# Prompt attention: the value product split over column halves of TensorE, its softmax sums over column quarters

## The reference

```python
s = jnp.einsum('bqgrd,bgqnjd->bgrqnj', qb, kg)          # selected blocks
p = masked_softmax(s - slopes * dist, m_s, axes=(-2, -1))
o_s = jnp.einsum('bgrqnj,bgqnjd->bqgrd', p, vg)
...
p_w = masked_softmax(s_w - slopes * dist_w, m_w, axes=-1)  # window of 512
o_w = jnp.einsum('bgrqk,bkgd->bqgrd', p_w, vwb)
...
o = gt[..., 0:1] * o_c + gt[..., 1:2] * o_s + gt[..., 2:3] * o_w
```

## Time and profile before

| | us |
|---|---|
| Median of 3 runs | 2069.13 (2068.73 to 2072.95) |
| Profiled execution, its own time | 2070.01 |
| Its span in the profile | 2068.1 |
| TensorE busy | 1850.6 (89% of the span) |
| VectorE busy | 866.3 (42%) |
| ScalarE busy | 541.1 (26%) |
| Mean granted clock | 0.938 |
| Value product L1939, 128 keys, busy | 139.9 |

### The profile page before, as it was taken

One profiled execution on the slowest core, in us unless ns is written; L12 is line 12 of the kernel. 1 busy time (PEld: TensorE's weight loads), 2 busy tenths in 40 slices (PEclk: granted clock), 3 DMA queues, 4 the chain that ended last, 5 costly groups with the idle time before them and its releaser, 6 DMA issues. The chain is left out here.

```text
span 2068.1 us, 27935 instructions
## 1 busy us (share of the span) xinstructions
PE 1850.6 (89%) x11698; PEld 1576.6 (76%) x11698; DVE 866.3 (42%) x1540; ACT 541.1 (26%) x1001; POOL 223.7 (11%) x285
## 2 busy tenths in 40 slices
PE   2799989948887687899999898899999999999997
PEld 2798889937777675555555687899999999999996
DVE  4634161123333434454443453444444444444446
ACT  3221221132222124444444322211211111122112
POOL 0200000022232101001100000100011011110000
PEclk9999999969999666999999999999999999999999
DMA  4000013030000200000000301111111111111102
GB/s 120 23 24 30 13 53 133 15 95 2 2 2 29 62 1 25 1 1 21 21 0 1 127 1 41 62 41 41 41 43 60 41 41 41 41 41 41 41 31 87
DMA packets 31503, 79.50 MB, mean 38 GB/s; under 512 B 11390, under 2 KB 17870, under 8 KB 26098
## 3 DMA queue, kind: packets, MB, share of 16 engines
q1 hardware_dynamic: 31314, 77.63, 11.1%
q0 software_dynamic: 64, 0.09, 0.0%
HBM read 69.62 MB, written 10.12 MB: 39 GB/s over the span
## 5 line engine op out<-in xcount | busy, mean ns | idle before, releaser
L266 PE MATMUL ps<-mix_hi,wbuf 128*128 128x364 f32 (+1 forms) x768 | 254.1, 331 | 9.5 <-DVE wbuf L2703 6.1
L267 PE MATMUL ps<-mix_lo,wbuf 128*128 128x364 f32 (+1 forms) x768 | 253.6, 330 | 0.0
L268 PE MATMUL ps<-mix_hi,wbuf 128*128 128x364 f32 (+1 forms) x768 | 253.6, 330 | 0.0
L2739 DVE TENSOR_TENSOR x<-x,ps 128x512 f32<-128x512 f32 (+1 forms) x288 | 190.6, 684 | 120.2 <-PE ps L268 120.2
L266 PE MATMUL ps<-wbuf,mlp_hid_hi 128*128 128x512 f32 x576 | 225.3, 391 | 4.4 <-DVE wbuf L2703 4.4
L267 PE MATMUL ps<-wbuf,mlp_hid_hi 128*128 128x512 f32 x576 | 225.2, 391 | 0.0
L268 PE MATMUL ps<-wbuf,mlp_hid_lo 128*128 128x512 f32 x576 | 225.0, 391 | 0.0
L2725 DVE TENSOR_TENSOR mlp_hid_lo<-mlp_rect,mlp_hid_hi 128x364 fp32r<-128x364 f32 (+1 forms) x96 | 75.2, 783 | 290.0 <-ACT mlp_hid_hi L2646 290.0
L266 PEld LDWEIGHTS ps<-mix_hi,wbuf 128*128 128x128 f32 x768 | 146.2, 190 | 10.5 <-DVE wbuf L2703 6.4
L2697 POOL TENSOR_TENSOR mlp_rect<-mlp_rect 128x364 f32<-128x364 f32 (+1 forms) x96 | 76.0, 791 | 661.3 <-ACT mlp_rect L2668 661.3
L267 PEld LDWEIGHTS ps<-mix_lo,wbuf 128*128 128x128 f32 x768 | 145.8, 190 | 0.5
(11 more groups left out here) (536 smaller groups left out, 3494.2 us busy)
## 6 DMA issues: line engine op xcount, KB each, us to landing
out_raw<-in_w_up SPq DMA_DIRECT2D x16, 1024.0 KB, 4.8
mlp_raw_down<-in_w_down SPq DMA_DIRECT2D x16, 1024.0 KB, 4.8
feat_raw<-in_w_feat SPq DMA_DIRECT2D x12, 512.0 KB, 5.0
spare<-in_w_token SPq DMA_DIRECT2D x4, 1056.0 KB, 5.2
ln_x<-in_x_prompt SPq DMA_DIRECT2D x8, 512.0 KB, 4.1
ck<-in_cache_nsa SPq DMA_DIRECT2D x16, 256.0 KB, 3.0
out_raw<-in_w_out SPq DMA_DIRECT2D x4, 1024.0 KB, 4.8
x<-in_x_prompt SPq DMA_DIRECT2D x8, 512.0 KB, 6.1
```

What stands on the lines that cost most here:

```text
L266: pe.matmul(out, lhs[0], rhs[0], start=first, stop=False)
L267: pe.matmul(out, lhs[0], rhs[1], start=False, stop=False)
L268: return pe.matmul(out, lhs[1], rhs[0], start=False, stop=last)
L2739: dve.tensor_tensor(part, part, m.ps[:n, u % 8, :], ALU.add).then_inc(added, 1)
```

## The change

- The value tiles lose their column of ones: `vaug` and `vcaug` become `v_all` and `v_blocks`, 64 columns wide. A tile `ones` of 32 columns is added.
- The value product becomes two products of 256 moving columns with the same 64-column stationary operand. Heads 0 and 1 go to output partitions 0 to 63, heads 2 and 3 to partitions 64 to 127, both in columns 0 to 255 of the bank.
- The sums become four products of 128 moving columns with the 32-column `ones`. Head `h` goes to partitions 32h to 32h + 31, in columns 256 to 383 of the same bank.
- ScalarE copies 128 x 384 out of the bank in place of 65 x 512. The tail has three transposes of 128 x 128 in place of four of 65 x 128. VectorE's four operations keep their sizes and read other places.

```diff
-                    pe.matmul(m.ps[:VW, 5 + br, :], v, PT[st % PTN][:k, :], start=first,
-                              stop=s == branch_end(n, br)).then_inc(pv_step, 1)
+                    bank, probs, done = m.ps[:, 5 + br, :], PT[st % PTN], s == branch_end(n, br)
+                    for z in range(2):
+                        pe.matmul(bank[64 * z:64 * z + 64, 0:2 * P], v, probs[:k, 2 * z * P:2 * (z + 1) * P], start=first,
+                                  stop=done, skip_group_check=True)
+                    for h in range(R):
+                        last = pe.matmul(bank[SUMW * h:SUMW * (h + 1), 2 * P:3 * P], ones[:k, :], probs[:k, h * P:(h + 1) * P],
+                                         start=False, stop=done, skip_group_check=True)
+                    last.then_inc(pv_step, 1)
...
-                        for h in range(R):
-                            last = pe.transpose(bank[:, h * VW:(h + 1) * VW], oT[b][:, h * P:(h + 1) * P], m.ident[:VW, :VW])
+                        for c in range(3):
+                            last = pe.transpose(bank[:, c * P:(c + 1) * P], oT[b][:, c * P:(c + 1) * P], m.ident[:])
...
-                    act.activation(oT[b], m.ps[:VW, 5 + b, :], ACT.Copy).then_inc(evac[b], 1)
+                    act.activation(oT[b], m.ps[:, 5 + b, 0:3 * P], ACT.Copy).then_inc(evac[b], 1)
...
-                        dve.tensor_tensor(part[:, n % 2, b], heads[:, :, 0:HD], fac[:, b, :].unsqueeze(2).to_broadcast([P, R, HD]),
+                        dve.tensor_tensor(part[:, n % 2, b].rearrange("p (z c) d -> p z c d", z=2), values,
+                                          fac[:, b, :].rearrange("p (z c) -> p z c", z=2).unsqueeze(3).to_broadcast([P, 2, 2, HD]),
                                           ALU.mult).then_inc(reduced, 1)
```

More of the change, by code:

```diff
@@ L1700, in prompt_attention @@
         Q0, Qa, Qb = (sb(n, [P, 2, 512], F32R) for n in ("Q0", "Qa", "Qb"))
-        VW = HD + 1
-        vaug, vcaug = sb("vaug", [P, TS, 2, G, VW]), sb("vcaug", [16, G, VW])
+        SUMW = P // R
+        v_all, v_blocks, ones = sb("v_all", [P, TS, 2, G, HD]), sb("v_blocks", [16, G, HD]), sb("ones", [P, SUMW])
         ident_r, mask, mask_c = sb("ident_r", [P, P], F32R), sb("mask", [P, 2, P], F32R), sb("mask_c", [16, TS, P], F32R)
@@ L1708, in prompt_attention @@
         PT = [m.kv[:, t, 0:512] for t in range(PTN)]
-        oT = [m.kv[0:VW, PTN + b, 0:512] for b in range(3)]
+        oT = [m.kv[:, PTN + b, 0:384] for b in range(3)]
         stage = part[:].rearrange("p a b r d -> p (a b r d)")
@@ L1818, in _ @@
                 value = Link(pool, v_ready)
-                value(pool.memset(vaug[:, :, :, :, HD:], 1.0))
-                value(pool.memset(vcaug[:, :, HD:], 1.0))
+                value(pool.memset(ones[:], 1.0))
                 for br, col in ((SEL, VSEL), (WIN, VWIN)):
-                    value(pool.tensor_copy(vaug[:, :, br, :, 0:HD],
+                    value(pool.tensor_copy(v_all[:, :, br, :, :],
                                            m.kv[:, 0:TS, col:col + P].rearrange("p t (g d) -> p t g d", g=G)))
-                value(pool.tensor_copy(vcaug[:, :, 0:HD], m.vc[:].rearrange("p (g d) -> p g d", g=G)))
+                value(pool.tensor_copy(v_blocks[:], m.vc[:].rearrange("p (g d) -> p g d", g=G)))
                 for n in range(UN):
@@ L1929, in multiply @@
                     br, t = steps(n)[s]
-                    k, v = (16, vcaug[:, g, :]) if br == CMP else (P, vaug[:, t, br, g, :])
+                    k, v = (16, v_blocks[:, g, :]) if br == CMP else (P, v_all[:, t, br, g, :])
                     st = first_step[n] + s
@@ L1935, in multiply @@
                         pe.wait_ge(keys_done, ALL_KEYS)
-                        pe.wait_ge(v_ready, 5)
+                        pe.wait_ge(v_ready, 4)
                     if first and n:
                         pe.wait_ge(evac[br], n)
-                    pe.matmul(m.ps[:VW, 5 + br, :], v, PT[st % PTN][:k, :], start=first,
-                              stop=s == branch_end(n, br)).then_inc(pv_step, 1)
+                    bank, probs, done = m.ps[:, 5 + br, :], PT[st % PTN], s == branch_end(n, br)
[6 more added lines that the diff above has]
+                    last.then_inc(pv_step, 1)
                 for g in range(G):
@@ L2021, in _ @@
                         elif st == 0:
-                            act.wait_ge(v_ready, 5)
+                            act.wait_ge(v_ready, 4)
                         act.activation(PT[st % PTN][:rows, :], m.ps[:rows, 3 + x % 2, :], ACT.Exp).then_inc(ring_out, 1)
@@ L2078, in work @@
                         i, g = units[n]
-                        heads = bank[:, 0:R * VW].rearrange("p (h n) -> p h n", h=R)
+                        sums = bank[:, 2 * P:3 * P].rearrange("p (h n) -> p h n", h=R)[:, :, 0]
+                        values = bank[:, 0:2 * P].rearrange("p (c z d) -> p z c d", c=2, z=2)
                         gates = m.small[:, i, 0:24].rearrange("p (h c) -> p h c", c=3)[:, R * g:R * g + R, (1, 2, 0)[b]]
-                        link(dve.tensor_scalar(rs[:, b, :], heads[:, :, HD], 1e-30, None, ALU.max))
+                        link(dve.tensor_scalar(rs[:, b, :], sums, 1e-30, None, ALU.max))
                         link(dve.reciprocal(fac[:, b, :], rs[:, b, :]))
```

## The result

The changed kernel takes 2097.3 us (median of 4 runs, 2094.87 to 2101.93) where the kernel before takes 2069.4: a ratio of 1.0134, 95% interval 1.0113 to 1.0155. It is slower by 28 us; the forecast was 2096.

What follows compares the result with a forecast made beforehand. TensorE was taken to bound the kernel. Against the profiled 2070.0 us: steps +34.5, pooled steps -4, tails +4.5, turns -8, clock -1, together +26, so 2096 us; range 2076 to 2116, some 80%.

Steps and rivals of the forecast that it cites:

- What bounds: In prompt attention TensorE sets the pace, busy 315 of 337 us, so a step's cost is paid almost in full.
- The streams: In a step's value part, halves and quarters side by side stream in 0.65 us in place of 0.86.
- The quarters: In the sums, four 32-column products run together and stream in 0.22 us; no row showed quarters together.
- Three changes at 0.14, 0.12 and 0.19: Per step, TensorE's shape changes with loads, in us: 128 to 64 columns, 64 to 32, and 32 to 128.
- A step: Each of 132 steps of 128 keys gets 0.26 us longer, +34.5 in all.
- A pooled step: Each of 16 pooled steps, already paying two shape changes, takes 0.94 us for 1.19, -4 in all.
- The turns: TensorE's waits for VectorE's scaling between units shrink, each of 15 turns giving back 0.55 us: -8.
- the -1 of the sum: In steps at the lower clock level the saved streaming is worth twice as much: -1 us, a guess.
- the hidden changes: Rival: in the value products' row shape changes are hidden and only streams count, so 2048 us; 5%.
- serial quarters: Rival: the sums' quarters run two at a time, 2128 us (8%), or one at a time, 2192 us (4%).
- the free middle change: Rival: the change from 64 to 32 columns in each step costs nothing, 18 us less: 2078 us; 7%.
- the 15 us of its rival: Rival: idle gaps make the granted clock drop, 30 us more at the lower level costing some 15: 2111 us; 10%.

Runs made afterwards that it cites:

- the kernel with one quarter: The changed kernel with all four 32-column sum products sent to partitions 0 to 31: 2173.5 us, ratio 1.0509.
- sums on halves: The changed kernel with the sums as two 64-column products of 256 columns in place of four 32-column ones, copy and tail fitted: 2104.6 us, ratio 1.0173.
- the kernel without sums: The changed kernel without the four 32-column products for the softmax sums: 2050.6 us, ratio 0.9913.
- the column less: The kernel before with a value product of 64 stationary columns for 65, sums left out, copy and transposes of 64 rows: 2106.2 us, ratio 1.0181.
- the one that holds the first product back: The changed kernel with value products held and run in batches of three, a unit's first product held too, 72 groups for 148: 2088.9 us, ratio 1.0096.
- up to three steps to a group: The changed kernel with value products held and run in groups, a unit's first one at once, 82 groups for 148: 2070.5 us, ratio 1.0010.
- up to five: The changed kernel with held value products in groups of up to five steps, a unit's first at once, two more exponential slots, 66 groups: 2060.8 us, ratio 0.9960.

## Why the prediction was right

- *What bounds.* TensorE did. The copy in ScalarE got 0.1 shorter and VectorE's work stayed, and the time moved with TensorE's step alone.
- *The streams.* 0.65 for 0.86 was right. The quarters, which rested on an analogy with halves, are shown by the kernel with one quarter.
- *Three changes at 0.14, 0.12 and 0.19.* The step after shows 0.10 + 0.05, 0.09 + 0.03 and 0.09 + 0.10. The middle one, for which no row existed, is shown twice: by the 0.58 against 0.49 with sums on halves, and by the kernel without sums. The price in the shape rather than in the products is shown by the column less.
- *A step.* +0.26 was forecast; 0.28 was measured in the dense stretch. The 0.02 between them is 2.6 us over 132 steps. (132 times 0.26 is 34.3; the sum has 34.5.)
- *A pooled step.* From L1902 ahead of the two value products to L1917 behind them it is 2.73 us (1109.95 to 1112.68); before it was 2.72 (1090.32 to 1093.04). The forecast of 0.26 for the one and -0.25 for the other was right.
- *The turns.* Here the result of the step was right and its parts were not. The time from L1917 at 1112.68 to the release of L1886 at 1116.58 is 3.90 in the changed kernel; in the kernel before it was 4.00 (1093.04 to 1097.04). So the chain didn't depend on TensorE's work, and it got shorter by the 0.1 of the copy, as forecast. But the work in that stretch was to grow by 0.44 and the wait to shrink by 0.55 a turn, from 21 to some 13 us in all. The view of waits gives 16.5: 4.7 less, not 8. At this turn the wait went from 1.23 to 1.06 while the work from the first L1917 to the first L1886 behind it went from 2.31 to 2.36. The first value product and the tails hardly got longer. Before, that product already stood 0.31 behind L1918 in place of 0.23, waiting for its exponential, and took 0.92 to the next start; now it stands 0.33 behind and takes 0.94. The sum didn't suffer, since the chain sets the end of a turn whatever TensorE does in it: what the work was over-counted by, the wait gave back too much. The kernel before at this turn, then the changed one:

```profile
1093.81 0.40 PE L1918 MATMUL ps<-pa_Qb,pa_Kb 128*128 128x512 f32 x1
1094.12 1.07 PE L1939 MATMUL ps<-tokens,pa_vaug 128*65 128x512 f32 x2
...
1095.35 0.47 PE L1887 MATMUL ps<-pa_Ka,pa_Q 128*128 128x512 f32 x1
```

```profile
1112.68 0.39 PE L1917 MATMUL ps<-pa_Qb,pa_Kb 128*128 128x512 f32 x1
...
1113.11 0.60 ACT L2028 ACTIVATE tokens<-ps 128x512 f32<-128x512 f32 x1 [1.06 <-PE ps L1917]
...
1113.80 0.65 PE L1940 MATMUL ps<-tokens,pa_v_all 128*64 128x256 f32 x4
...
1114.74 0.55 PE L1864 MATMUL ps<-ident,tokens 128*128 128x128 f32 x3
1115.04 0.48 PE L1886 MATMUL ps<-pa_Ka,pa_Q 128*128 128x512 f32 x1
1116.58 0.50 PE L1886 MATMUL ps<-pa_Ka,pa_Q 128*128 128x512 f32 x1 [1.06 <-DVE pa_part L2092]
```

```profile
PE ps L1886 <- DVE pa_part L2092: 16.5, 20, 1.1
```

- *The clock.* The stage has 0.96 where it had 0.97. With two levels, one at half of the other, that is 0.08 of 365 us at the lower level where it was 0.06 of 337: by these rounded rows 29 us for 20, and the 9 more cost at most 4 to 5. So the -1 of the sum, which took the clock as a small gain, isn't borne out. The clock may make up what is left between 26 forecast and 28 measured, and so may the 0.02 a step; no run separates them.
- *Rivals.* The hidden changes, serial quarters and the free middle change are refuted by the runs above. The clock did not cost the 15 us of its rival in this kernel. In the one that holds the first product back it may have cost up to 12.

## What to carry to other kernels

Count the changes of the stationary operand's shape, not the array's idle columns. Here one costs 0.09 us before its load, an estimated 110 float32 columns in a pass, and there were three in each step of 1.83 us. Narrow products need runs of one shape to pay for that: with up to three steps to a group this kernel was within 0.1% of the one before, with up to five 0.4% faster. Widths of 64 and 65 are two shapes: trimming 65 to 64 cost 0.34 us a step here, more than a score product of 512 columns streams. Before moving work out of a stretch in which an engine waits, price the wait it was filling, and look at the granted clock behind it.

## What the runs showed of the hardware

The passes of products on different halves are interleaved. With four records a step, two a half, the first passes of both halves start together, then the second ones: 4 records fill 0.65, one record being 0.38 to 0.43 long, while on one half the four take 1.08. The trace doesn't name the pass of a record, so this is read from the starts alone.

The granted clock doesn't follow the length of the steps or of the stage. In the kernel with batches of three, waits of 1.27 and 0.84 us in a turn are followed by a grant of 0.54 over 3.7 us. The stage with the sums on one quarter, which has the longest steps, was granted 0.99, and so was the one with the sums on halves. Two stages of nearly one length differ: 323 us without the sums at 0.94, 329 us with five steps to a group at 0.98. What decides the grant stays open here. The stage with the sums on one quarter:

```profile
801.00:1244.00 443.00, 433.46 (x2711) 274.39 (x2711) 153.28 (x388) 142.45 (x254) 34.73 (x34) 0.99 0.02 6
```
